# A one-core hybrid decoder step: early modulation slabs that hold two tiles of shift and scale, smaller tables at the start, and a turned score product in the GLA heads

## The chip, the cores and the metric

One core of one Trainium2 chip runs the whole step. The metric is the time of one execution in microseconds (us); a kernel is given by the median of its runs.

## The reference, cut to what matters

```python
mod = silu(c) @ w_ada + b_ada                      # c: 1 prompt row, 8 sample rows; w_ada 2048 x 12288
shift1, scale1, gate1, shift2, scale2, gate2 = split(mod, 6)
h = rmsnorm(x, norm1_g) * (1 + scale1) + shift1    # 256 prompt tokens, 32 sample tokens
qa, ka, va, qb, kb, vb, r, glr = split(h @ w_in)
oa = mix_a(...)                                    # dilated attention with a T5 relative bias, samples read a cache
ob = mix_b(...)                                    # 4 GLA heads: decay, causal product q k, states
x = x + gate1 * (concat(norm(oa), norm(ob) * silu(r)) @ w_out)
h2 = rmsnorm(x, norm2_g) * (1 + scale2) + shift2
x = x + gate2 * conv_ffn(h2)                       # w_up, causal conv, silu, w_down
```

Outputs are y for prompt and samples, the new keys and values, GLA states and conv rows. The depth is 1, and all is float32.

## The kernel before, in words

The program is written by hand for each engine: the order on an engine is the order of its code, and semaphores tie the engines. The 2048 features are 16 tiles of 128. Tokens (288 columns) are the moving operand of every large product; weights are split into a high part (`whi`, ScalarE) and a low part (`wlo`, VectorE), and `three` (lines 949 to 951) issues three matmuls per tile of weights. A chunk is 4 tiles by 256 columns of weights: 24 matmuls.

**The opening.** SyncE loads the constants `con` (identity, head halves, ones, then the masks `causal`, `causal_s`, `own_batch`, and `sum_groups`), x, and the first slabs of `w_ada`. TensorE turns x (`x_turns`, line 854), then works on slabs 0 to 7 of `w_ada` (`early_slab`), on the bias tables (`biases`, lines 862 to 866, from tables that GpSimd loads into `temp`), and between them on products of constants whose result nobody reads (`idle_products`, line 881). The small semaphore counts of a `Steps` object name each hand-over, and `upto` waits for one.

**Early slabs.** Shift and scale of the first norm come in 4 groups of 512 features each. Group i has 8 slabs of 1 MB: four of shift, four of scale, each with 4 of the 16 tiles by 512 columns. In a slab the four tiles go to four groups of 32 array columns (`ada_slab`, line 893), so that four partial sums lie on 4 x 32 PSUM rows. `ada_rows` (line 1507) copies 512 columns to `mrow`, and `ada_turn` (line 907) multiplies by `sum_groups`, which adds the four parts and turns them: 4 matmuls with 9 columns, once for shift (`turn_a`) and once for scale (`turn_b`). Then VectorE adds the bias (`mod`), scales the normalized tiles (`norm_group`) and splits them; with group 0 done the first chunk can start. Slabs 8 to 31 run between the first 20 chunks, where the table `ADA_AT` puts them. Slabs 12 to 31 are issued by ScalarE (`lead_load`, line 1524), each when an earlier slab is spent. The chunks' own loads come from SyncE (`in_load`, line 570). After chunk 20, late slabs (one tile by 2048 columns, `tile_slab`, line 900) carry the other four sixths of `w_ada`.

**ScalarE's loop** does per chunk j: copies of old results, `in_hi(j + 3)` (line 1488, waits for the slab of `w_in` and a free buffer), slab loads, row copies, then its part of a head or a pair.

**GLA heads.** Four heads run beside chunks 28 to 60; `head(h, r)` is step r of head h on each engine, a step per chunk. In steps 4 and 5 TensorE makes the causal products of 8 stretches of 32 queries: `att(h, c)` has the keys `ki[c]` as the weights and 32 query columns as the moving operand, in one matmul (line 1039) or, from c = 4, two (lines 1039 and 1042), so that they come out with keys on rows. VectorE multiplies them by `causal` (line 2163) in step 6. TensorE adds squares in step 8 (line 1119), after all eight new states are done; line 1061 starts the next head.

**GpSimd** loads the small tables first, waits for the third group's turn, and then loads `wglr`, `wg2` and the first states (lines 742 to 752).

## Time and profile before

| | |
|---|---|
| median of 3 runs | 1621.52 us (1619.14 to 1622.28) |
| the profiled execution's own time | 1621.12 us |
| its span | 1619.6 us |
| TensorE busy | 1582.2 us, 98% of the span |
| VectorE, ScalarE, GpSimd busy | 890.9, 664.2, 76.9 us |
| moved by DMA | 370.81 MB, mean 229 GB/s |
| share of the chain that ended last | PE 83%, DMA 5%, issue 5%, DVE 4%, ACT 2% |
| granted TensorE clock, mean | 0.994 |

Times in the profile count from the start of the span. A matmul of float32 has two records (two passes), so an "x8" is 4 matmuls of the program. A record ends when its pipeline has drained, so two that follow each other overlap; the cost of a group on a busy TensorE is from its start to the start of what follows.

### The profile page before, as it was taken

The page shows a single profiled execution, that of the slowest core. Times are in us where ns is not written, and L with a number is a line of the kernel's source. Part 1 is how long each engine was busy: PE and PEld are TensorE (multiplying, and loading weights), DVE is VectorE, ACT ScalarE, POOL GpSimd, SP SyncE. Part 2 cuts the span into 40 slices and gives each one's busy share as a digit, 9 for nine tenths or more (in the row PEclk, how much of TensorE's full clock was granted, in tenths as well). Part 3 has the DMA queues.
Part 4 walks back from the last instruction along what each step waited for, and adds up shares of the span by engine and source line. Part 5 has one row for each costly group of instructions (what it writes and reads, how often), then busy time and mean ns, then how long its engine had stood idle before and what let it go on. Part 6 is the DMA issues. An engine that isn't in the chain of part 4 may idle for free.

```text
span 1619.6 us, 29366 instructions
## 1 busy us (share of the span) xinstructions
PE 1582.2 (98%) x12352; PEld 1430.2 (88%) x12352; DVE 890.9 (55%) x1504; ACT 664.2 (41%) x925; POOL 76.9 (5%) x135
## 2 busy tenths in 40 slices
PE   8899999999999998999999999999999999999997
PEld 4677888888877765997999999999999999999997
DVE  3555555555665654657445455454555556656563
ACT  3332333343445434435334333343433445545452
POOL 2010000000111000000000000000000000000000
PEclk8999999999999999999999999999999999999999
DMA  9998877778877999866644444555545455555450
GB/s 339 375 384 298 307 258 260 270 278 282 288 255 278 335 397 368 310 231 235 229 163 158 158 161 156 182 163 175 161 158 168 148 170 179 160 177 179 158 183 27
DMA packets 240881, 370.81 MB, mean 229 GB/s; under 512 B 7809, under 2 KB 192483, under 8 KB 232553
## 3 DMA queue, kind: packets, MB, share of 16 engines
q1 hardware_dynamic: 216032, 279.88, 51.1%
q10 hardware_dynamic: 17538, 71.45, 11.8%
q0 software_dynamic: 7184, 17.64, 3.3%
q8 instruction: 98, 1.61, 0.4%
q14 instruction: 29, 0.24, 0.0%
HBM read 359.06 MB, written 9.88 MB: 228 GB/s over the span
## 4 chain that ended last, share of the span: by engine, by line
PE 83%; DMA 5%; issue 5%; DVE 4%; ACT 2%; SPq 1%; POOL 0%; ACTq 0%; POOLq 0%; DVEq 0%
PE ps L949 23%; PE ps L950 22%; PE ps L951 22%; PE ps L900 3%; PE ps L1197 2%; DMA ring<-in_w_in 1%; DMA ring<-in_w_ada 1%; DMA vals<-in_w_ada 1%; SPq L548 1%; DMA proj<-in_w_ada 1%; DVE wlo L2041 1%; PE ps L1212 1%; PE ps L1243 1%; PE ps L893 1%; DMA ring<-in_w_out 1%
## 5 line engine op out<-in xcount | busy, mean ns | idle before, releaser
L949 PE MATMUL ps<-hhi,whi 128*128 128x288 f32 x3120 | 929.7, 298 | 1.7 <-DVE hlo L2033 0.7
L950 PE MATMUL ps<-hlo,whi 128*128 128x288 f32 x3120 | 917.8, 294 | 0.0
L951 PE MATMUL ps<-hhi,wlo 128*128 128x288 f32 x3120 | 917.6, 294 | 0.0
L949 PEld LDWEIGHTS ps<-hhi,whi 128*128 128x128 f32 x3120 | 586.0, 188 | 40.1 <-issue 35.3
L950 PEld LDWEIGHTS ps<-hlo,whi 128*128 128x128 f32 x3120 | 586.2, 188 | 0.8
L951 PEld LDWEIGHTS ps<-hhi,wlo 128*128 128x128 f32 x3120 | 586.0, 188 | 0.0
L1897 DVE TENSOR_TENSOR wlo<-ring,whi 128x1024 fp32r<-128x1024 f32 x178 | 212.2, 1221 | 84.7 <-ACT whi L1479 84.3
L1479 ACT ACTIVATE whi<-ring 128x1024 fp32r<-128x1024 f32 x178 | 184.5, 1056 | 156.3 <-PE ps L951 156.3
L2041 DVE TENSOR_TENSOR wlo<-ring,whi 128x1024 fp32r<-128x1024 f32 x96 | 117.2, 1223 | 124.2 <-ACT whi L1488 124.0
L1488 ACT ACTIVATE whi<-ring 128x1024 fp32r<-128x1024 f32 x96 | 100.8, 1054 | 157.5 <-PE ps L951 125.4
L2541 DVE TENSOR_TENSOR wlo<-ring,whi 128x1024 fp32r<-128x1024 f32 (+1 forms) x94 | 105.7, 1131 | 56.0 <-ACT whi L1817 56.0
L1817 ACT ACTIVATE whi<-ring 128x1024 fp32r<-128x1024 f32 (+1 forms) x94 | 91.8, 980 | 73.8 <-PE ps L951 73.7
L2459 DVE TENSOR_TENSOR hlo<-proj,hhi 128x1152 fp32r<-128x1152 f32 (+3 forms) x56 | 60.9, 1100 | 47.5 <-ACT hhi L1766 46.6
L1766 ACT ACTIVATE hhi<-proj 128x1152 fp32r<-128x1152 f32 (+3 forms) x56 | 52.7, 954 | 49.7 <-PE ps L951 49.7
L2480 DVE TENSOR_SCALAR work<-work,small 128x304 f32<-128x304 f32 x44 | 17.3, 436 | 99.2 <-ACT work L1778 99.2
L2492 DVE TENSOR_TENSOR proj<-ps,work 128x512 f32<-128x512 f32 x22 | 15.2, 692 | 84.5 <-PE ps L951 84.5
L1777 ACT ACTIVATE work<-ps 128x512 f32<-128x512 f32 x22 | 13.2, 599 | 109.2 <-PE ps L951 109.2
L900 PE MATMUL ps<-ring,c 128*32 128x512 f32 x416 | 50.2, 599 | 0.0
L2298 DVE COPY kcT<-ps 128x512 f32<-128x512 f32 x40 | 27.3, 690 | 35.0 <-PE ps L1197 35.0
L1677 ACT ACTIVATE whi<-ring 128x1024 fp32r<-128x1024 f32 x30 | 30.9, 1052 | 35.4 <-DMA ring<-in_w_out 24.3
L2483 DVE SCALAR_TENSOR_TENSOR work<-work,small 128x304 f32<-128x304 f32 x88 | 43.2, 532 | 1.6
L1197 PEld LDWEIGHTS ps<-con,ring 128*128 128x128 f32 x320 | 34.8, 140 | 8.3 <-issue 4.8
(318 smaller groups left out, 1115.7 us busy)
## 6 DMA issues: line engine op xcount, KB each, us to landing
ring<-in_w_up SPq DMA_DIRECT2D x88, 1024.0 KB, 5.1
ring<-in_w_ada ACTq DMA_DIRECT2D x58, 1024.0 KB, 7.2
ring<-in_w_in SPq DMA_DIRECT2D x48, 1024.0 KB, 8.8
ring<-in_w_down SPq DMA_DIRECT2D x32, 1408.0 KB, 6.6
ring<-in_cache_k_win SPq DMA_DIRECT2D x16, 1024.0 KB, 9.3
ring<-in_w_out SPq DMA_DIRECT2D x16, 1024.0 KB, 7.0
proj<-in_w_ada SPq DMA_DIRECT2D x14, 1024.0 KB, 9.4
ring<-in_w_ada SPq DMA_DIRECT2D x10, 1024.0 KB, 13.6
```

Source lines behind the costliest of these rows:

```text
L900: last = mm(ps[32 * g:32 * g + 32, bank, :], c32[:, k, :], rows[:, 512 * g:512 * g + 512], start=(k == 0), stop=(k == KD - 1))
L949: mm(out, w_hi, x_hi, start=start, stop=False)
L950: mm(out, w_hi, x_lo, start=False, stop=False)
L951: return mm(out, w_lo, x_hi, start=False, stop=stop)
L1197: last = turn(ps[:, 2 * (n % 2) + e, P * q:P * q + P], key_slab(t)[:, i // 2, c:c + P], ident)
L1479: f(whi[:, j % BUFS, 0:n], ring[:, s % SLOTS, n * (j % 2):n * (j % 2) + n], ACT.Copy).then_inc(hi_done, 1)
L1488: f(whi[:, j % BUFS, :].rearrange("p (k c) -> p k c", k=4), in_chunk_of(rows, j), ACT.Copy).then_inc(hi_done, 1)
L1817: f(whi[:, jj % BUFS, 0:n], ring[:, s % SLOTS, CHUNK * kc:CHUNK * kc + n], ACT.Copy).then_inc(hi_done, 1)
L1897: v.tensor_tensor(wlo[:, j % BUFS, 0:n], ring[:, s % SLOTS, n * (j % 2):n * (j % 2) + n], whi[:, j % BUFS, 0:n].bitcast(F32), ALU.subtract ...
L2041: v.tensor_tensor(wlo[:, j % BUFS, :].rearrange("p (k c) -> p k c", k=4), in_chunk_of(rows, j), whi[:, j % BUFS, :].bitcast(F32).rearrange ...
L2459: last = v.tensor_tensor(hlo[:, at:at + m, :], actT[:, k0:k0 + m, :], hhi[:, at:at + m, :].bitcast(F32), ALU.subtract)
L2541: v.tensor_tensor(wlo[:, jj % BUFS, 0:n], ring[:, (2 * kg + h) % SLOTS, CHUNK * kc:CHUNK * kc + n], whi[:, jj % BUFS, 0:n].bitcast(F32), A ...
```

## The change

Seven edits:

1. Slab s of a group now holds tiles 2(s mod 8) and 2(s mod 8) + 1, each with 512 columns of shift and 512 of scale. It comes in two DMAs, one per tile, with a semaphore each. TensorE makes 8 matmuls with 256 columns instead of 4 with 512; each group of 32 array columns has a stretch of its own (shift left, shift right, scale left, scale right) and adds over all 16 tiles. So there is one copy of 256 columns and one turn of 2 matmuls with 36 columns per group, in place of two copies of 512 and two turns of 4 matmuls with 9.
2. SyncE loads only the first 384 columns of `con`; the 424 columns of masks are loaded by GpSimd, after the fourth group's turn, ahead of `wglr`. GpSimd's wait for the third group becomes one for the fourth.
3. 640 columns of `mult_s` on 128 rows become 4 rows (`mult_t`) and a 4-row table that spreads them (`pick_t`); two more matmuls add them in PSUM, and VectorE copies where it added.
4. ScalarE's loop issues slab loads before `in_hi(j + 3)`, and late rows before both.
5. `att` has the 32 queries as the weights and up to 256 key columns as the moving operand: one matmul for each stretch, on its own 32 PSUM rows. ScalarE copies the 384 columns, and TensorE turns them by three transposes (`att_turns`).
6. The squares of step 8 wait for six of the eight new states, and the next head's first product for all.
7. `gate_rank` and what hangs on it move by one chunk; the idle products before the up-projection are 2 instead of 6.

```diff
-        keep = CONST_LAYOUT["sum_groups"][0] + NC9
+        front, keep = CONST_LAYOUT["causal"][0], CONST_LAYOUT["own_batch"][0] + NB
+        w_shift = a["w_ada"][0].rearrange("(k p) (h c) -> p k h c", p=P, h=6)[:, :, 0:2, :]
+        def ada_source(s, e):
+            at = 512 * (s // 8)
+            return w_shift[:, 2 * (s % 8) + e, :, at:at + 512]
+                for e in range(2):
+                    sp.dma_start(rows[:, 2 * e:2 * e + 2, :], ada_source(s, e)).then_inc(landed_in[e], 16)
-            sp.dma_start(con[:, :], a["tables"][:, 0:keep]).then_inc(con_in, 16)
+            sp.dma_start(con[:, 0:front], a["tables"][:, 0:front]).then_inc(con_in, 16)
...
+            pool.dma_start(temp[0:TS, ct - c0:c1 - c0], a["tables"][0:TS, ct:c1]).then_inc(temp_in, 16)
-            pool.wait_ge(*AT.upto("turn_b", 2))
+            pool.wait_ge(*AT.upto("turn", 3))
             pool.wait_ge(fill_c, 1)
+            pool.dma_start(con[:, front:keep], a["tables"][:, front:keep]).then_inc(masks_in, 16)
...
-                mm(ps[:, 1, :], rel_rows, tview("hot_s", P)[:, 0:512], start=True, stop=True)
+                mm(ps[:, 1, :], rel_rows, tview("hot_s", P)[:, 0:512], start=True, stop=False)
+                mm(ps[:, 1, :], tview("pick_t", TS), tview("mult_t", TS)[:, 0:512], start=False, stop=True)
...
+            def early_slab(s):
+                for e in range(2):
+                    k = 2 * (s % 8) + e
+                    pe.wait_ge(landed_in[e], landed)
+                    for g in range(4):
+                        c = 256 * (g % 2)
+                        last = mm(ps[32 * g:32 * g + 32, rows_at, 0:256], c32[:, k, :], rows[:, 2 * e + g // 2, c:c + 256],
+                                  start=(k == 0), stop=(k == KD - 1))
+            def early_turn(i):
+                for n in range(2):
+                    last = mm(out[:, :, n, :], mrow[:, P * n:P * n + P], nines, start=True, stop=True)
...
-                q = qp[:, 32 * c:32 * c + 32]
-                n = min(P, 32 * (c + 1))
-                last = mm(ps[0:n, 7, 32 * c:32 * c + 32], ki[c % 4][:, 0:n], q, start=True, stop=True)
-                if c >= 4:
-                    n = 32 * (c - 3)
-                    last = mm(ps[0:n, 7, P + 32 * c:P + 32 * c + 32], ki[c % 4][:, P:P + n], q, start=True,
-                              stop=True)
+                at, n, rows = P * (c // 4), 32 * (c + 1), slice(32 * (c % 4), 32 * (c % 4) + 32)
+                mm(ps[rows, 7, at:at + n], qp[:, 32 * c:32 * c + 32], ki[c % 4][:, 0:n], start=True,
+                   stop=True).then_inc(*RT.step(f"att{c}"))
+            def att_turns(h):
+                pe.wait_ge(*RA.upto("att_rows", h))
+                for n in range(3):
+                    last = turn(ps[:, 7, P * n:P * n + P], att_rows[:, P * n:P * n + P], ident)
...
+                    pe.wait_ge(*RV.upto("state1", h - 1))
                     mm(ps[:, 7, 0:TOK], wg2[:, P * h:P * h + P], glrT, start=True, stop=True).then_inc(*RT.step("z"))
...
-                    pe.wait_ge(*RV.upto("state1", h))
+                    pe.wait_ge(*RV.upto("state_half", h))
...
-                    idle_products(2, 6)
+                    idle_products(2, 2)
```

TensorE, from slab 4 to the first chunk (line 862 and on are the bias products; `vals` holds slabs 4 to 7), before:

```order
L893 MATMUL ps<-vals,c 32x512 x4
L862 MATMUL ps<-proj 16x512
L865 MATMUL ps<-proj 128x512
L866 MATMUL ps<-proj 128x160
L907 MATMUL ps<-con,mrow 128x9 x4
L893 MATMUL ps<-vals,c 32x512 x8
L881 MATMUL ps<-con 128x256 x3
L893 MATMUL ps<-vals,c 32x512 x4
L881 MATMUL ps<-con 128x256
L907 MATMUL ps<-con,mrow 128x9 x4
L881 MATMUL ps<-con 128x256 x8
```

and changed:

```order
L927 MATMUL ps<-vals,c 32x256 x8
L878 MATMUL ps<-proj 16x512
L881 MATMUL ps<-proj 128x512
L882 MATMUL ps<-proj 128x512
L883 MATMUL ps<-proj 128x32
L884 MATMUL ps<-proj 128x128
L885 MATMUL ps<-proj 128x128
L927 MATMUL ps<-vals,c 32x256 x16
L900 MATMUL ps<-con 128x256 x3
L927 MATMUL ps<-vals,c 32x256 x8
L900 MATMUL ps<-con 128x256
L937 MATMUL ps<-con,mrow 128x4x9 x2
```

The turn behind the bias products is gone, one matmul with 512 columns and one with 128 are added there, and the last turn has 2 matmuls.

ScalarE, from its first chunk of the loop (line 1488 is `in_hi`, 1524 the slab load, 1536 a copy of a result), before:

```order
L1536 ACTIVATE proj<-ps 128x288
L1488 ACTIVATE whi<-ring 128x1024
L1524 DMA ring<-in_w_ada 128x4x512
L1536 ACTIVATE proj<-ps 128x288
L1488 ACTIVATE whi<-ring 128x1024
L1524 DMA ring<-in_w_ada 128x4x512
L1524 DMA proj<-in_w_ada 128x4x512
```

and changed:

```order
L1549 ACTIVATE proj<-ps 128x288
L1538 DMA ring<-in_w_ada 128x2x512 x2
L1505 ACTIVATE whi<-ring 128x1024
L1549 ACTIVATE proj<-ps 128x288
L1538 DMA ring<-in_w_ada 128x2x512 x2
L1538 DMA proj<-in_w_ada 128x2x512 x2
L1505 ACTIVATE whi<-ring 128x1024
```

Each slab load stands ahead of the `whi` of its chunk, and is two DMAs.

TensorE, step 5 of a head (line 1089 and on are the state and the samples' rows), before:

```order
L1039 MATMUL ps<-proj 128x32
L1042 MATMUL ps<-proj 96x32
L1039 MATMUL ps<-proj 128x32
L1042 MATMUL ps<-proj 128x32
L1089 MATMUL ps<-proj 128x256
L1090 MATMUL ps<-proj 128x256
L1094 MATMUL ps<-ring 32x256 x8
```

and changed:

```order
L1052 MATMUL ps<-proj 32x160
L1052 MATMUL ps<-proj 32x192
L1052 MATMUL ps<-proj 32x224
L1052 MATMUL ps<-proj 32x256
L1106 MATMUL ps<-proj 128x256
L1107 MATMUL ps<-proj 128x256
L1111 MATMUL ps<-ring 32x256 x8
L1059 MATMUL ps<-con,proj 128x128 x3
```

Eight small products became four wider ones, and three transposes stand at the end of the step.

## Rows read from the trace of the kernel before

**Rows 1.** The page: busy time, share of the span and instructions of each engine.

```profile
PE 1582.2 (98%) x12352; PEld 1430.2 (88%) x12352; DVE 890.9 (55%) x1504; ACT 664.2 (41%) x925; POOL 76.9 (5%) x135
```

**Rows 2.** Waits of TensorE, whole span: us in total, times, longest.

```profile
PE ps L893 <- DMA proj<-in_w_ada: 3.1, 3, 1.7
PE ps L893 <- DMA ring<-in_w_ada: 2.4, 2, 1.4
...
PE ps L1119 <- DVE ring L2107: 1.5, 2, 0.7
```

**Rows 3.** Stretches: us, PE, PEld, DVE, ACT, POOL busy, PEclk, DMA share, GB/s.

```profile
58.20:62.00 3.80, 3.80 (x30) 2.80 (x29) 2.71 (x4) 3.80 (x6) 0.00 (x0) 1.00 0.76 254
112.00:116.00 4.00, 4.00 (x36) 3.56 (x28) 1.69 (x4) 1.30 (x3) 0.00 (x0) 1.00 1.05 386
124.00:128.00 4.00, 4.00 (x31) 3.00 (x31) 1.69 (x4) 1.29 (x2) 0.00 (x0) 1.00 1.02 269
152.00:156.00 4.00, 4.00 (x33) 4.00 (x32) 3.23 (x10) 1.22 (x3) 0.00 (x0) 1.00 0.24 90
```

**Rows 4.** DMA issues up to 150 us: count, KB each, median us to landing.

```profile
proj<-in_tables POOLq DMA_DIRECT2D x1, 720.0 KB, 8.1
con<-in_tables SPq DMA_DIRECT2D x1, 408.5 KB, 3.7
```

**Rows 5.** Timeline of TensorE, slab 4 to the first chunk: start us, us.

```profile
31.63 1.06 PE L893 MATMUL ps<-vals,c 128*32 128x512 f32 x8 [2.25 <-DMA vals<-in_w_ada]
32.63 1.03 PE L862 MATMUL ps<-proj 32*16 32x512 f32 x2
...
34.82 0.95 PE L907 MATMUL ps<-con,mrow 128*128 128x9 f32 x8
...
37.63 1.56 PE L881 MATMUL ps<-con 128*128 128x256 f32 x6
39.31 1.06 PE L893 MATMUL ps<-vals,c 128*32 128x512 f32 x8
...
41.18 1.03 PE L907 MATMUL ps<-con,mrow 128*128 128x9 f32 x8 [0.18 <-ACT mrow L1507]
...
46.44 0.37 PE L949 MATMUL ps<-hhi,whi 128*128 128x288 f32 x1 [0.68 <-DVE hlo L2033]
```

**Rows 6.** Timeline of ScalarE, the high part of chunk 4.

```profile
58.20 1.06 ACT L1488 ACTIVATE whi<-ring 128x1024 fp32r<-128x1024 f32 x1 [7.91 <-DMA ring<-in_w_in]
```

**Rows 7.** Timeline of TensorE, a slab at 137 us.

```profile
137.11 1.07 PE L893 MATMUL ps<-ring,c 128*32 128x512 f32 x8 [1.38 <-DMA ring<-in_w_ada]
```

**Rows 8.** Timeline of TensorE, a late turn.

```profile
270.36 0.98 PE L977 MATMUL ps<-con,mrow 128*128 128x36 f32 x8
```

**Rows 9.** Timeline of TensorE in the sample attention.

```profile
543.10 1.07 PE L1212 MATMUL ps<-kcT,proj 128*32 128x256 f32 x16
543.98 0.48 PE L1225 MATMUL ps<-qkS,proj 128*32 128x32 f32 x32
544.39 1.97 PE L1197 MATMUL ps<-con,ring 128*128 128x128 f32 x16
546.29 1.07 PE L1212 MATMUL ps<-kcT,proj 128*32 128x256 f32 x16
```

**Rows 10.** Timeline of TensorE, steps 4 and 5 of the first head.

```profile
201.23 0.97 PE L1039 MATMUL ps<-proj 128*32 128x32 f32 x8
...
206.00 0.30 PE L1039 MATMUL ps<-proj 128*128 128x32 f32 x2
...
207.84 0.68 PE L1089 MATMUL ps<-proj 128*128 128x256 f32 x2
```

**Rows 11.** Timeline of VectorE, the keys of step 5.

```profile
205.08 1.23 DVE L2103 TENSOR_TENSOR proj<-proj 128x160 f32<-128x160 f32 x4
```

**Rows 12.** Timeline of TensorE, chunk 3 of the up-projection.

```profile
767.63 0.37 PE L949 MATMUL ps<-hhi,whi 128*128 128x288 f32 x1 [0.42 <-DVE wlo L1897]
```

**Rows 13.** A stretch at its start, columns as in rows 3.

```profile
750.00:755.00 5.00, 5.00 (x34) 4.74 (x33) 4.96 (x15) 3.02 (x7) 0.00 (x0) 1.00 1.01 421
```

More of the change, by code:

```diff
@@ L114, in constants @@
         new.append(np.where(b[:, None] == a[None] // TS, m, NEG))
-    add("mult_s", np.concatenate([old] + new, 1).astype(np.float32))
+    add("mult_s", np.concatenate(new, 1).astype(np.float32))
     return np.concatenate(parts, 1)
@@ L339, in build @@
         NL = [st("norm1_lower", "l0", "l1", "l2", "l3"), st("norm2_lower", "l0", "l1", "l2", "l3")]
-        AT = st("ada_tensor", "turn_a", "turn_b")
-        AA = st("ada_scalar", "rows_a", "rows_b")
+        AT = st("ada_tensor", "turn")
+        AA = st("ada_scalar", "rows")
         AV = st("ada_vector", "mod")
@@ L483, in out_slab, with ada_place @@
             return t % SLOTS, t // SLOTS * 16 + 16 - EVEN_LESS
+        half_in = [sem(f"slot_half_in{t}") for t in range(SLOTS)]
+        first_half = [sem(f"first_slab_half_in{t}") for t in range(4)]
+        lead_half = [sem(f"lead_slab_half_in{t}") for t in range(2)]
+        def ada_place(s):
+            place, slot, landed = ada_home(s)
+            rows = slab(slot, 4, 512) if place == 0 else (first_rows, lead_rows)[place - 1][slot]
+            return rows, ((full, first_in, lead_in)[place][slot], (half_in, first_half, lead_half)[place][slot]), landed
+        def ada_source(s, e):
+            at = 512 * (s // 8)
+            return w_shift[:, 2 * (s % 8) + e, :, at:at + 512]
         ADA_AT = [0, 1, 1, 2, 3, 3, 4, 5] + [6 + 7 * s // 8 for s in range(8)] + [13 + 7 * s // 8 for s in range(8)]
@@ L543, in ada_load @@
             def ada_load(s):
-                i, at = s // 8, 512 * (s // 8) + D * (s // 4 % 2)
-                place, slot, _ = ada_home(s)
-                dst = slab(slot, 4, 512) if place == 0 else (first_rows, lead_rows)[place - 1][slot]
-                sp.dma_start(dst, w_ada[:, 4 * (s % 4):4 * (s % 4) + 4, at:at + 512]
-                             ).then_inc((full, first_in, lead_in)[place][slot], 16)
+                rows, landed_in, _ = ada_place(s)
+                for e in range(2):
+                    sp.dma_start(rows[:, 2 * e:2 * e + 2, :], ada_source(s, e)).then_inc(landed_in[e], 16)
             def half_load(w, s, column, slot):
@@ L888, in norm2_sum @@
                 last.then_inc(*NT[1].step(f"s{n}"))
-            def ada_slab(bank, s, rows):
-                for k in range(4):
-                    last = mm(ps[32 * k:32 * k + 32, bank, :], c32[:, 4 * (s % 4) + k, :], rows[:, k, :],
-                              start=(s % 4 == 0), stop=(s % 4 == 3))
-                last.then_inc(raw_used, 1)
             def tile_slab(bank, k, rows):
@@ L902, in tile_slab @@
                 last.then_inc(raw_used, 1)
[L904 to L923 removed]
+            def early_slab(s):
+                i, rows_at = s // 8, 7 if s // 8 % 2 else 3
+                if i and s % 8 == 0:
+                    pe.wait_ge(*AA.upto("rows", i - 1))
+                rows, landed_in, landed = ada_place(s)
+                for e in range(2):
[5 more added lines that the diff above has]
+                                  start=(k == 0), stop=(k == KD - 1))
+                last.then_inc(raw_used, 1)
+            def early_turn(i):
+                pe.wait_ge(*AA.upto("rows", i))
+                pe.wait_ge(*AV.upto("mod", i - 1))
+                pe.sem_inc(row_turns, 1)
+                out = ps[:, 5, 0:8 * NC9].rearrange("p (g n c) -> p g n c", g=4, n=2)
+                for n in range(2):
+                    last = mm(out[:, :, n, :], mrow[:, P * n:P * n + P], nines, start=True, stop=True)
+                last.then_inc(*AT.step("turn"))
             idle_products(6, 6)
@@ L1518, in lead_load @@
             def lead_load(a):
-                place, slot, _ = ada_home(8 + a)
-                dst = slab(slot, 4, 512) if place == 0 else lead_rows[slot]
-                at = 512 * (1 + a // 8) + D * (a // 4 % 2)
+                rows, landed_in, _ = ada_place(8 + a)
                 act.wait_ge(raw_used, a + 5)
-                act.dma_start(dst, w_ada[:, 4 * (a % 4):4 * (a % 4) + 4, at:at + 512]
-                              ).then_inc(full[slot] if place == 0 else lead_in[slot], 16)
+                for e in range(2):
+                    act.dma_start(rows[:, 2 * e:2 * e + 2, :], ada_source(8 + a, e)).then_inc(landed_in[e], 16)
             def late_load(r):
@@ L2179, in head @@
                         last = new_state(b)
+                        if b == 5:
+                            last.then_inc(*RV.step("state_half"))
                     last.then_inc(*RV.step(f"state{r - 7}"))
```

110 lines of the change are left out of this document (48 added, 62 removed).

## The prediction

> **What bounds the kernel now.** I read the page first: TensorE is busy for 98% of the span [rows 1]. Time that leaves its stream after the opening is therefore gained, if nothing it waits for comes later, and a faster ScalarE or VectorE alone gains nothing. The list of its waits comes next: after the first product the longest are for slabs of `w_ada`, 3.1 + 2.4 = 5.5 us [rows 2], all before 140 us; the other that the change touches is 1.5 us for the GLA states. The stretches say why the slabs are late: the DMA engines are full (share 1.05 at 386 GB/s at 112 us), lose rate beside GpSimd's small packets (269 GB/s at 124 us), and have nothing to do from 152 us on (share 0.24) [rows 3]. So there are three regimes: an opening that ends with a latency chain, 95 us in which DMA and TensorE are nearly equal, and TensorE alone after that.
>
> **The start of the first chunk.** SyncE's constants shrink from 408.5 KB to 384 columns x 128 rows x 4 bytes = 192 KB, GpSimd's table from 720 KB to 400 KB plus 12 KB for the rows of 4 [rows 4]. That is 0.53 MB less ahead of slab 7, at 386 GB/s [rows 3] 1.4 us. Slab 4, which waited for its load until 31.63 [rows 5], starts 1.4 us earlier. From there to slab 7 TensorE has its own queue: it ended its idle products at 37.63 + 1.56 = 39.2 and slab 7 began at 39.31, so TensorE was only just ahead of the load. In that queue a turn goes (0.88 us, as long as the one between 34.82 and slab 5) and a matmul of 512 columns (0.96, from 32.63 to the next) and one of 128 (about 0.27) come. Slab 7 starts 1.4 + 0.88 - 0.96 - 0.27 = 1.1 us earlier, and its load no longer decides. Behind it the copy has 256 columns instead of 512 and the turn 2 matmuls instead of 4: the wide turn's 8 records last 0.98 against 0.95 for the narrow one's [rows 8, 5], so the price is by the matmul, and half a turn is 0.44 us. With 0.2 for the copy (an estimate) this gives 0.6. VectorE's work from the turn to the first product (46.44) [rows 5] stays. First chunk: **1.7 us** earlier, between 0.9 (if slab 7 keeps its slack) and 2.2.
>
> **From there to chunk 21.** TensorE's share: after the first group there were six turns of 0.88, now three of 0.44: 5.3 - 1.3 = 4.0 us. The slabs themselves I take at no change. The nearest row has exactly the new form, 128x32 weights and 256 columns in four groups of array columns: 16 records from 543.10 to 543.98, 0.88 us [rows 9], where a slab's 8 records of 512 columns take 1.00 (31.63 to 32.63). DMA's share: the 1.4 us of bytes, and a hole. From 58.2 to 62 us the engines moved 254 GB/s [rows 3], 1.3 us lost, because ScalarE stood 7.91 us before the `whi` of chunk 4, waiting for `w_in` [rows 6], with the slab loads behind it. Edit 4 puts them ahead. So up to about 90 us the loads gain 1.4 + 1.3 = 2.7, and TensorE, which could gain 1.7 + 1.3, is held to 2.7. After 90 us it waited once more, 1.38 us at 137 us [rows 7], when GpSimd's loads had thinned the stream. These move behind the fourth turn (about 143 us), next to the stretch in which DMA is nearly idle. There the 0.22 MB of masks and 1.2 MB of `wglr`, gates and states need some 6 us of DMA time, which 152 to 160 us have free; nothing of it is used before `gate_rank`, now at chunk 25, some 20 us later. So this wait goes, and four of the six old turns lie here, two of the new: 3.5 - 0.9 = 2.6. Sum up to chunk 21: 2.7 + 2.6 + 1.4 = **6.7 us**. Bounds: 1.4, only the bytes; and 1.7 + 4.0 + 5.5 = 11.2, every wait gone.
>
> **The heads.** Step 4's products took 0.8 us (0.97 with the drain), step 5's 1.84 (206.00 to 207.84) [rows 10]: 2.64 us. New: 320 moving columns in step 4, 832 in step 5. At 1024 columns in 0.88 us [rows 9], four groups at once, these are 0.27 and 0.72. Three transposes are 6 records; 16 such took 544.39 to 546.29 [rows 9], so 0.71. Together 1.70, a gain of 0.94 per head, **3.8 us** for four. The keys don't hold it: VectorE had made the last at 206.31 [rows 11]. ScalarE's new copy of 384 columns lies beside 2 us of other products, and VectorE's masking, which starts some 1 us later, ends long before step 6. Other bound: if the groups did not overlap, 1152 columns x 4 x 0.86 ns = 4.0 plus 0.7 is 2.0 more than before, a loss of 8 us.
>
> **The states.** The waits of line 1119 [rows 2] go: two new states fewer are awaited, some 0.8 us by VectorE, and the next head's first product stands behind the sum, which covers it. **1.5 us**, at worst 0.
>
> **Costed at nothing.** VectorE's copies replace additions of the same size. Four idle products fewer: TensorE then meets the normalized tiles as they come. VectorE is busy 4.96 of 5 us there [rows 13], and TensorE already had to wait for it at 767.63 [rows 12], so what starts earlier waits longer. If that cover is gone it is 1.7 us. ScalarE's doubled issues are covered by its 59% of idle time.
>
> **A rule against the change.** Every early slab becomes two DMAs of 512 KB. The rows here have 1 MB slabs at 386 GB/s [rows 3], in queues that are never empty, so that an end of one DMA lies beside another; I take the same rate for halves. The Trainium skill ("DMA: Bandwidth & Descriptors", Bandwidth) says to batch DMAs to 1 MiB or more to reach 75% of peak, and gives 138 GB/s for 64 KB; by that the slabs would come more slowly; the third rival below prices that with numbers of this kernel. No run here shows 512 KB halves with these 2 KB pieces.
>
> Sum: 6.7 + 3.8 + 1.5 = 12.0 us off the profiled execution's 1621.1, 1609.1; the median of the runs shown is 0.4 above that execution, so **1609.5 us**.
>
> **Rivals.**
> - *The loads keep the opening.* The two-queue order helps one side and hurts the other, or the masks and states now hit the loads of chunks 22 to 26; up to chunk 21 only 1.4 us come. For it: DMA is full until 150 us. Against: the hole at 58 us and the empty stretch at 152. 1609.5 + 5.3 = 1614.8. Chance 0.17.
> - *The head products don't overlap.* Their widths differ, and each waits for its own keys. For it: 8 us of loss as above, in place of 3.8. Against: the row of equal form [rows 9]. 1609.5 + 11.8 = 1621.3, no change. Chance 0.05.
> - *Halved DMAs cost* (the Trainium skill's rule above, as a mechanism of this kernel). 32 DMAs more before 137 us. The loads have 2.7 us and the 5 us of GpSimd's thinned stretch to spare, and 5.3 are gained later; the result turns to slower by 0.2% when each extra DMA costs over (7.7 + 5.3 + 3.2) / 32 = 0.5 us. At 0.7 us they cost 22: 1621.5 + 22 - 13 = 1631. Against: the full queues. Chance 0.03.
> - *The change acts as stated*, within 4 us of the sum. Chance 0.75.
>
> **How the numbers follow.** A measurement tells 0.2%, 3.2 us, from no change. Faster by that: 0.75 + 0.17 = 0.92, less 0.01 for a half-clock stretch; same 0.06; slower 0.03. The low end is the bound of 11.2 in place of 6.7, 1605; the high end takes in the first rival with a quarter off its heads and states, 1617. Beyond are the other two, and a rest.
>
> **What would show it.** First chunk at 44.7 us; a turn of 4 records for each group, about 0.44 us; slabs of 16 records in 0.9 to 1.0 us; DMA over 370 GB/s from 56 to 62 us; no wait near 137 us; chunk 21 some 6.7 us earlier. Steps 4 and 5 of a head 1.7 us with the transposes; no wait of the sum for states. Slabs of over 1.2 us, or a DMA rate under 350 GB/s from 60 to 110 us, would make it wrong.

## The result and the profile after

The changed kernel is **0.2% slower**: 1624.44 us median (1620.14 to 1628.16, 20 runs) against 1620.73 for the kernel before (1618.34 to 1623.72, 20 runs), ratio 1.0021 with a 95% interval of 1.0015 to 1.0028. The forecast was 1609.5, range 1605 to 1617. Its profiled execution took 1623.34 us, span 1621.8.

The page of the changed kernel, busy times:

```profile
PE 1578.5 (97%) x12538; PEld 1429.9 (88%) x12538; DVE 890.0 (55%) x1504; ACT 662.5 (41%) x925; POOL 78.1 (5%) x137
```

TensorE has 3.7 us less to do than in [rows 1], and the span is 2.2 us longer (1619.6 before), so it stands idle for 5.9 us more. The waits of TensorE in the changed kernel say for what (total, times, longest, in us):

```profile
PE ps L963 <- DVE hlo L2047: 4.3, 2, 3.6
PE ps L900 <- DMA con<-in_tables: 4.0, 1, 4.0
PE ps L963 <- ACT proj L1549: 2.7, 1, 2.7
PE ps L1178 <- DVE proj L2226: 2.7, 2, 1.8
PE ps L1169 <- DVE proj L2267: 2.2, 2, 1.1
...
PE ps L1145 <- DVE proj L2223: 1.9, 2, 0.9
...
PE ps L927 <- DMA ring<-in_w_ada: 1.2, 2, 0.7
```

The waits for the slabs of [rows 2] fell from 5.5 us to 1.2, and the wait of the sum for the GLA states is gone. In their place TensorE waits for *computed* data: a copy by ScalarE, `hlo` of the second feature group, and intermediate results of the pairs.

To see where the difference arises I take the start of the first product of a chunk. Every kernel has the same 24 products per chunk in the same order, so chunk n of one stands against chunk n of another. In us from the span's start:

| chunk | before | changed | changed - before |
|---|---|---|---|
| 0 | 46.44 | 44.55 | -1.89 |
| 3 | 60.33 | 61.27 | +0.94 |
| 6 | 79.08 | 75.17 | -3.90 |
| 8 | 89.89 | 91.31 | +1.42 |
| 21 | 150.88 | 149.83 | -1.05 |
| 61 | 359.70 | 355.68 | -4.03 |
| 64 | 372.45 | 368.42 | -4.03 |
| 98 | 639.98 | 642.33 | +2.35 |
| 384 | 1583.17 | 1585.48 | +2.31 |

Two places give away what the rest gains: the two stalls up to chunk 8, and the stretch with the pairs, chunks 64 to 98, which takes 6.4 us longer, 5.2 of them by chunk 93.

**The stall before chunk 8.** ScalarE, VectorE and TensorE in the changed kernel (timeline: start, us, engine, line, operation; in brackets the idle time before it and what ended it):

```profile
80.97 4.96 ACTq L1538 DMA_DIRECT2D ring<-in_w_ada  x4
86.03 1.06 ACT L1505 ACTIVATE whi<-ring 128x1024 fp32r<-128x1024 f32 x1 [6.58 <-issue]
```

```profile
87.12 1.23 DVE L2055 TENSOR_TENSOR wlo<-ring,whi 128x1024 fp32r<-128x1024 f32 x1 [6.61 <-ACT whi L1505]
88.27 0.29 DVE L1939 TENSOR_TENSOR modT<-ps,small 128x36 f32<-128x36 f32 x2
...
90.72 1.56 DVE L2047 TENSOR_TENSOR hlo<-proj,hhi 128x288 fp32r<-128x288 f32 x4
```

```profile
91.31 0.58 PE L963 MATMUL ps<-hhi,whi 128*128 128x288 f32 x1 [3.56 <-DVE hlo L2047]
```

ACTq is ScalarE's queue at its DMA issues. Four half slabs took 4.96 us to issue, ahead of `whi` for chunk 10. VectorE makes `wlo` for chunk 10 before it scales feature group 1, so it stood 6.61 us, and TensorE, which at chunk 8 needs group 1 and not chunk 10's weights, waited 3.56 us. It then got the lower of its two clocks, 1.2 GHz, for a time: two successive stretches of the changed kernel, the columns as in [rows 3] (the granted clock, 0.86 and 0.71, is the third number from the end):

```profile
88.00:92.00 4.00, 0.69 (x3) 0.72 (x4) 3.83 (x14) 1.81 (x6) 0.00 (x0) 0.86 1.05 386
92.00:96.00 4.00, 4.00 (x23) 3.85 (x22) 1.86 (x3) 0.98 (x1) 0.00 (x0) 0.71 1.05 386
```

Chunk 8 took 91.31 to 97.01, 5.70 us against 4.35 before: 1.3 us more. In the kernel before, the same loads stood behind `whi` and were two issues in 1.23 us.

**The stall before chunk 3.** The splitting of chunk 4, which stood at 58.20 in [rows 6], comes at 59.77, and the copy that frees chunk 3's PSUM bank is behind it:

```profile
59.77 1.06 ACT L1505 ACTIVATE whi<-ring 128x1024 fp32r<-128x1024 f32 x1 [11.37 <-DMA ring<-in_w_in]
...
60.73 0.39 ACT L1549 ACTIVATE proj<-ps 128x288 f32<-128x288 f32 x1
```

In the four kernels with the early loads ahead (changed, and 3, 4 and 8 below) this splitting starts at 59.8 to 60.9 us, in those with the loads behind, where it waits for `w_in` too, at 57.0 to 58.2. That slabs issued from 49 us on take DMA time from this `w_in` fits, but no run separates it. The hole at 58.2 to 62 us did get smaller (309 GB/s against 254), but most of that is not of edit 4: with it undone (kernel 1 below) the engines moved 293 GB/s there.

**The pairs.** What ScalarE waited for between 375 and 500 us, first in the kernel before, then in the changed one:

```profile
ACT whi L1488 <- PE ps L951: 24.4, 10, 5.0
```

```profile
ACT whi L1505 <- PE ps L912: 16.6, 5, 5.4
ACT whi L1505 <- PE ps L965: 12.0, 6, 3.6
...
ACT mrow L1514 <- PE ps L912: 1.5, 1, 1.5
```

Line 912 is the product of a late slab. Before, the splitting waited only for its own buffer (line 951, or 965 after the change). Now a late load stands ahead of it, and waits for a slab's products, which TensorE does behind the 24 products of a chunk. ScalarE's part of the pair, and VectorE's behind it, come later with the splitting, and TensorE's waits for them (lines 1178, 1169 and 1145 in the list above) grow.

### The profile page after: what moved, and what is told of

Its sections match the earlier page's. It is cut to its first block, busy times and chain, and to the rows that moved or that the text cites. A ratio compares the mean times of both kernels' runs of the same rounds, so it can differ in the third digit from the quotient of the medians.

```text
span 1621.8 us, 29765 instructions
## 1 busy us (share of the span) xinstructions
PE 1578.5 (97%) x12538; PEld 1429.9 (88%) x12538; DVE 890.0 (55%) x1504; ACT 662.5 (41%) x925; POOL 78.1 (5%) x137
## 4 chain that ended last, share of the span: by engine, by line
PE 81%; DMA 6%; issue 5%; DVE 4%; ACT 2%; SPq 1%; ACTq 0%; POOL 0%; DVEq 0%; POOLq 0%
PE ps L963 23%; PE ps L964 22%; PE ps L965 22%; PE ps L912 3%; DMA proj<-in_cache_v_win 2%; DMA ring<-in_w_in 1%; PE ps L1214 1%; PE ps L927 1%; DVE wlo L2055 1%; DMA ring<-in_w_ada 1%; ACT whi L1505 1%; DMA vals<-in_w_ada 1%; SPq L563 1%; PE ps L1229 1%; PE ps L1260 1%
## 5 line engine op out<-in xcount | busy, mean ns | idle before, releaser
L2476 DVE TENSOR_TENSOR hlo<-proj,hhi 128x1152 fp32r<-128x1152 f32 (+3 forms) x56 | 60.9, 1100 | 47.5 <-ACT hhi L1780 46.5
```

The costliest lines, as they stand in the source:

```text
L2476: last = v.tensor_tensor(hlo[:, at:at + m, :], actT[:, k0:k0 + m, :], hhi[:, at:at + m, :].bitcast(F32), ALU.subtract)
```

## The experiments

My theory from these rows, A: **edit 4, the new order in ScalarE's loop, makes the splitting of `w_in` late and costs 10 to 12 us, and the rest of the change gains about what was forecast.** Rivals: the doubled number of DMA issues (edit 1) costs it wherever they stand; or the new work of heads and pairs (edits 5 and 6) shifted the later stretch. Each kernel was timed beside runs of the kernel before, not all in one session; here is what came of them, in us (medians; chunk starts are of the one profiled execution of each):

| kernel | median | ratio to before, 95% | chunk 8 | 21 | 61 | 64 | 98 |
|---|---|---|---|---|---|---|---|
| before | 1620.2 to 1621.7 | 1 | 89.89 | 150.88 | 359.70 | 372.45 | 639.98 |
| changed | 1624.44 | 1.0021 (1.0015-1.0028) | 91.31 | 149.83 | 355.68 | 368.42 | 642.33 |
| 1 order undone | 1611.86 | 0.9940 (0.9926-0.9955) | 89.37 | 146.54 | 351.21 | 363.96 | 630.80 |
| 2 early loads back | 1621.12 | 0.9998 (0.9989-1.0007) | 89.56 | 146.75 | 352.42 | 365.17 | 640.52 |
| 3 late loads, rows back | 1616.21 | 0.9966 (0.9955-0.9977) | 92.72 | 149.87 | 354.59 | 367.33 | 634.58 |
| 4 order alone | 1630.44 | 1.0055 (1.0041-1.0068) | 90.64 | 150.15 | 361.60 | 374.34 | 647.54 |
| 5 heads alone | 1617.65 | 0.9981 (0.9972-0.9991) | 89.61 | 150.91 | 355.52 | 368.27 | 632.46 |
| 6 halves alone | 1623.56 | 1.0020 (1.0011-1.0029) | 89.91 | 153.18 | 361.86 | 374.61 | 642.89 |
| 7 rows ahead | 1614.12 | 0.9962 (0.9949-0.9975) | 88.13 | 145.31 | 350.05 | 362.80 | 630.04 |
| 8 one burst back | 1610.84 | 0.9937 (0.9924-0.9950) | 89.60 | 146.78 | 351.52 | 364.27 | 632.17 |
| 9 late loads one later | 1616.91 | 0.9984 (0.9973-0.9996) | 90.25 | 147.43 | 359.43 | 372.18 | 640.38 |
| 10 GpSimd at the third | 1618.07 | 0.9983 (0.9974-0.9992) | 89.50 | 151.53 | 356.11 | 368.86 | 635.47 |
| 11 six idle products | 1612.07 | 0.9948 (0.9934-0.9961) | 89.86 | 147.04 | 352.05 | 364.80 | 634.55 |

**How far one trace can be read.** The profiled execution lies up to 4.5 us from the median of its kernel (kernel 9: 1621.42 against 1616.91; kernel 5: 1613.92 against 1617.65). Where that comes from can be seen. Up to chunk 8 the kernels 1, 2, 7, 9 and 11 run the same program, and start it at 88.13 to 90.25 us. Chunks 93 to 98 hold the attention of the samples, and take 114.4 to 120.0 us whatever the edit. Between these two places most chunks of the same program repeat to 0.01 us, except for chunk 41 (8.1 to 8.5 us in the kernels 1, 3, 7, 8, 10 and 11): chunks 8 to 21 take 57.15 to 57.18 in seven of the variants. So a difference in the opening or behind chunk 93 needs more than 2 us to count, and one in the middle does not. The pairs are best read from chunk 64 to 93: 149.7 to 150.7 us in the ten kernels in which no late load waits ahead of the splitting, against 154.97 (changed), 156.57 (kernel 4) and 158.40 (kernel 2).

**1. The order undone.** In the changed kernel, ScalarE's loop:

```diff
-                if j - 1 in LATE_AT[KD - 1::KD]:
-                    late_rows(LATE_AT.index(j - 1) // KD)
+                if j + 3 < CH_OUT:
+                    in_hi(j + 3)
...
-                if j + 3 < CH_OUT:
-                    in_hi(j + 3)
...
+                if j - 1 in LATE_AT[KD - 1::KD]:
+                    late_rows(LATE_AT.index(j - 1) // KD)
                 for h in range(H_B):
```

> The changed kernel with edit 4 alone undone: ScalarE's loop splits w_in (in_hi) first, issues the slab loads behind it, and copies late rows at its end, as the kernel before does. Theory A (the new order makes the splitting of w_in late, by loads in front of it in ScalarE's queue, and costs 10 to 12 us that hide the gain of the rest): about 1613 us, ratio to before 0.995; the wait of PE before chunk 8 for hlo (3.6 us) and the one for the projection copy before chunk 3 (2.7 us) gone, and chunks 64 to 98 take as long as before (they lose 6.4 us to it in the changed kernel). Rival B (twice as many DMA issues on ScalarE and in the rings cost it, wherever they stand): 1619 to 1624, ratio 0.999 to 1.002. Rival C (the loss in chunks 64 to 98 is of the heads' and pairs' new work, edits 5 and 6): chunks 64 to 98 still lose 6 us, about 1618.

Measured: 1611.86 us, 9.8 below the kernel before of the same runs and 12.6 below the changed one. Chunks 64 to 98 take 266.84 us, against 267.53 before and 273.91 in the changed kernel. The waits of TensorE up to 150 us, with the order undone:

```profile
PE ps L900 <- DMA con<-in_tables: 4.1, 1, 4.1
PE ps L870 <- DMA proj<-in_x_sample: 2.1, 1, 2.1
PE ps L927 <- DMA ring<-in_w_ada: 0.9, 1, 0.9
PE ps L927 <- DMA proj<-in_w_ada: 0.9, 2, 0.7
PE ps L963 <- DVE hlo L2047: 0.7, 1, 0.7
```

The 3.6 and the 2.7 us are gone, and `hlo` is back to the 0.7 that it had before. Theory A as stated holds; both rivals had named other numbers. (In this execution TensorE waited 2.1 us for the sample tokens, and chunk 0 began at 48.95. By chunk 8 it was at 89.37, as early as kernel 2, whose chunk 0 began at 45.04: what the start gains or loses hardly reaches chunk 8.)

**2 and 3. The two halves of edit 4.** Kernel 2 is the changed one with `lead_load`'s loop moved behind `in_hi`. Kernel 3 keeps it ahead, and puts `late_load` and `late_rows` where they were:

```diff
-                for a_ in range(4, 24):
-                    if ADA_AT[a_ - 4] == j - 1:
-                        lead_load(a_)
...
                 if j + 3 < CH_OUT:
                     in_hi(j + 3)
+                for a_ in range(4, 24):
+                    if ADA_AT[a_ - 4] == j - 1:
+                        lead_load(a_)
```

> The changed kernel with only the early slabs' loads put back behind the splitting of w_in; late loads and late rows stay ahead of it. Theory A: the opening's stalls at chunks 3 and 8 go (chunk 21 starts 5 to 6 us earlier than in the changed kernel), the loss from chunk 64 to 98 stays: about 1618 to 1619, ratio 0.998 to 0.999. Rival B: chunk 21 no earlier than 149.8, about 1624.

> The changed kernel with the late loads put back behind the splitting of w_in and the late rows at the loop's end; the early slabs' loads stay ahead. Theory A: chunk 21 starts as in the changed kernel (149.8), but chunks 64 to 98 take no longer than before: about 1618, ratio 0.998. Rival C: 1624, the chunks from 64 on lose 6 us as in the changed kernel.

Measured: 1621.12 and 1616.21, where I had 1618 to 1619 and 1618. The places are as expected, the sizes not: kernel 2 brings chunk 21 forward by 3.1 us, where I had said 5 to 6, and keeps the loss of the pairs (275.35 us for chunks 64 to 98); kernel 3 starts chunk 21 at 149.87 and does the pairs in 267.25. So the early loads ahead cost some 4 us, the late loads and rows some 9 (1616.21 and 1621.12 less 1611.86), 13.6 by themselves and 12.6 together.

**4. The order alone**, the same edit in the kernel before.

> The kernel before with edit 4 alone: slab loads and late rows ahead of the splitting of w_in in ScalarE's loop, nothing else changed. Theory A: 1626 to 1632, ratio 1.004 to 1.007, with waits of PE for hlo or the projection copy in the opening and a loss of some 6 us in chunks 64 to 98. Rival B (the halved loads' issues cost it, not their place): within 2 us of before, ratio 0.999 to 1.001. My forecast's own reading of edit 4 (a hole at 58 to 62 us closed, 1.3 us): 1620, ratio 0.999.

Measured: 1630.44, 8.7 us *slower* than before, in the range of theory A. Chunks 64 to 98 take 273.20 us, 5.7 more, and chunks 21 to 61 2.6 more. But chunk 21, at 150.15, starts 0.7 us *earlier* than before: the same early loads ahead of the splitting made chunk 3 start 2.0 us later and chunk 8 0.75, and by chunk 21 nothing of it was left. The burst at the same place, ScalarE in kernel 4:

```profile
82.31 2.95 ACTq L1524 DMA_DIRECT2D ring<-in_w_ada  x2
85.36 1.06 ACT L1488 ACTIVATE whi<-ring 128x1024 fp32r<-128x1024 f32 x1 [4.45 <-PE ps L893]
```

Two issues took 2.95 us, the four of the changed kernel 4.96, and TensorE waited 1.0 us at most for `hlo`, not 3.6. `whi` itself came only 0.7 us later in the changed kernel (86.03 against 85.36), and so did chunk 8; TensorE had got there earlier (chunk 6 at 75.17 against 77.03), so it stood longer, and chunk 8 at the lower clock took 5.70 us against 4.32. So the order alone explains the loss in the pairs. The one in the opening needs more of the change beside it: the halved DMAs, which lengthen the burst, and whatever brings TensorE there earlier. A kernel with the order and the halves only was not run.

**6. The halves alone.** In the kernel before, each early slab in two DMAs:

```diff
-                act.dma_start(dst, w_ada[:, 4 * (a % 4):4 * (a % 4) + 4, at:at + 512]
-                              ).then_inc(full[slot] if place == 0 else lead_in[slot], 16)
+                act.dma_start(dst[:, 0:2, :], w_ada[:, k:k + 2, at:at + 512]
+                              ).then_inc(full[slot] if place == 0 else lead_in[slot], 16)
+                act.dma_start(dst[:, 2:4, :], w_ada[:, k + 2:k + 4, at:at + 512]
+                              ).then_inc(half_in[slot] if place == 0 else lead_half[slot], 16)
```

(and the same on SyncE, and a second wait ahead of the products).

> The kernel before with every early slab loaded by two transfers of half the bytes (two tiles each, same rows and columns) on a semaphore each, and nothing else changed. Forecast and theory A: the bytes decide, not the number of transfers, and ScalarE's extra issues stand behind the splitting of w_in: 1620.5 to 1622.5, ratio 1.000. Rival B (the doubled issues cost it wherever they stand; forecast's rival priced it at some 10 us): 1625 or more, ratio 1.002 up.

Measured: 1623.56, 3.4 us slower than the 1620.17 of the kernel before in the same session. My range was missed; of the rival's two bounds the ratio of 1.002 was reached and the 1625 us not, so doubled issues do cost something by themselves. The halves alone do nothing to chunk 8 (89.91), and cost 2.6 us at one point, ahead of chunk 17. ScalarE and TensorE there:

```profile
127.71 3.99 ACTq L1535 DMA_DIRECT2D proj<-in_w_ada  x1
131.80 0.60 ACT L1515 ACTIVATE mrow<-ps 128x512 f32<-128x512 f32 x1 [4.40 <-issue]
```

```profile
132.54 1.03 PE L914 MATMUL ps<-con,mrow 128*128 128x9 f32 x8 [1.95 <-ACT mrow L1515]
...
134.91 0.61 PE L957 MATMUL ps<-hhi,whi 128*128 128x288 f32 x1
135.31 0.44 PE L958 MATMUL ps<-hlo,whi 128*128 128x288 f32 x1
135.55 0.44 PE L959 MATMUL ps<-hhi,wlo 128*128 128x288 f32 x1
```

One issue stood 3.99 us in the queue, with the row copy of a turn behind it, and after the wait the records follow each other at 0.24 us, where the full clock shows 0.13. In the kernel before, the one issue at that place took 0.37 us. So a doubled number of issues has a price where something urgent stands behind them on ScalarE. This place follows GpSimd's loads (117 to 122 us), as does the longest burst of kernel 10 below (two issues in 5.63 us at 125.74); with those loads moved to 147 us, kernel 1's two issues at 125.60 took 0.90. So part of the 3.4 us may be owed to GpSimd's loads, which the change moves away. The rate did not suffer: between 105 and 120 us the engines moved 381 GB/s in kernel 6 against 383 before, and 387 with the order undone, in a stream of halves of 512 KB and `w_in` slabs of 1 MB. By the Trainium skill's advice of DMAs of 1 MiB or more ("DMA: Bandwidth & Descriptors", Bandwidth) the slabs would have come more slowly; the measured rate does not bear that out here, and what the halves cost was time in the issuing queue.

**8. One burst back.** Kernel 3, but in the loop's step j = 7 (the four issues of 4.97 us) the early loads stand behind `in_hi`:

```diff
-                    if ADA_AT[a_ - 4] == j - 1:
+                    if ADA_AT[a_ - 4] == j - 1 and j != 7:
                         lead_load(a_)
                 if j + 3 < CH_OUT:
                     in_hi(j + 3)
+                for a_ in range(4, 24):
+                    if ADA_AT[a_ - 4] == j - 1 and j == 7:
+                        lead_load(a_)
```

> The changed kernel with late loads and late rows back behind the splitting of w_in, early loads ahead of it in every step of ScalarE's loop but the seventh, whose four issues of half a slab took 4.97 us ahead of the splitting for chunk 10. Theory A in its narrow form (that one burst makes the lower part of the second normalization group late by 3.6 us): chunk 8 starts some 3 us earlier than with all early loads ahead, total about 1613, against 1616.2 with the burst ahead and 1611.9 with all behind. If instead the loads ahead in the steps before it matter (they take DMA time from w_in), it stays at 1615 to 1616.

Measured: 1610.84; chunk 8 at 89.60, 3.1 us earlier than in kernel 3 (92.72). The stall before chunk 3 is still there (2.8 us), and the time is that of kernel 1 (ratio 0.9937 against 0.9940), where I had said about 1613. So, as far as the medians tell, this one burst was the whole of what the early loads cost. ScalarE in kernel 8:

```profile
82.38 1.06 ACT L1505 ACTIVATE whi<-ring 128x1024 fp32r<-128x1024 f32 x1 [1.00 <-DMA ring<-in_w_in]
82.89 4.97 ACTq L1538 DMA_DIRECT2D ring<-in_w_ada  x4
87.91 1.45 ACT L1480 ACTIVATE hhi<-proj 128x288 fp32r<-128x288 f32 x4 [4.47 <-DVE proj L2043]
```

The issues take as long as before, but `whi`, and with it VectorE's chain to `hlo`, is ahead of them.

**9. Late loads one chunk later.** Kernel 2 with

```diff
-                    if (LATE_AT[r - 2] if r >= 2 else ADA_AT[20 + r]) == j - 1:
+                    if (LATE_AT[r - 2] + 1 if r >= 2 else ADA_AT[20 + r]) == j - 1:
                         late_load(r)
```

> As the variant with early loads put back (late loads and late rows still ahead of the splitting of w_in), but each late load is issued one chunk later, when the slab whose buffer it takes has long been multiplied. Theory A, narrow form (the load waits on ScalarE for products that TensorE issues behind a head's or pair's work, and the splitting for three chunks on waits behind it): the 7.8 us lost between chunks 64 and 98 go, total 1611 to 1613, ratio 0.994 to 0.995. Rival (the loads' issue time or their traffic ahead of w_in costs it): as before this edit, 1619 to 1622. Rival C (chunks 64 to 98 slow down through the copy of late rows): also 1619 to 1622.

Measured: 1616.91, between the two. The stretch of the pairs, 64 to 93, takes 150.66 us, against 158.40 in kernel 2 and 150.12 in kernel 1: the loss there is gone, with the late loads still ahead of the splitting. It was the wait of the load that cost it, as the theory's narrow form says, and not the copy of late rows, which is ahead in both. But chunks 21 to 61 take 212.01 us where kernel 1 needs 204.68, which no theory had foreseen. This may overstate it: the profiled execution took 1621.42 us, and seven of the kernel's ten took 1616.07 to 1617.09, so part of the 7.3 us may belong to the slower executions only. The largest part, 3.3 us, falls in chunk 41. ScalarE, kernel 9 and then kernel 1:

```profile
244.17 1.06 ACT L1505 ACTIVATE whi<-ring 128x1024 fp32r<-128x1024 f32 x1 [5.46 <-DMA ring<-in_w_in]
245.13 1.53 ACT L1574 ACTIVATE proj<-proj 128x160 f32<-128x160 f32 x4
```

```profile
240.90 1.06 ACT L1505 ACTIVATE whi<-ring 128x1024 fp32r<-128x1024 f32 x1 [3.70 <-DMA ring<-in_w_in]
...
241.87 1.53 ACT L1574 ACTIVATE proj<-proj 128x160 f32<-128x160 f32 x4
```

The keys of a head's step 5 (line 1574) stand behind a splitting that waits for `w_in`, which lands later in kernel 9; TensorE waited 2.7 us for these keys, against 0.9 in kernel 1. Why `w_in` lands later there I have not separated (other loads at other times, or a `wlo` that frees its slot later).

**7. Rows ahead.** Kernel 1 with the copy of late rows ahead of `in_hi`:

```diff
+                if j - 1 in LATE_AT[KD - 1::KD]:
+                    late_rows(LATE_AT.index(j - 1) // KD)
                 if j + 3 < CH_OUT:
                     in_hi(j + 3)
...
-                if j - 1 in LATE_AT[KD - 1::KD]:
-                    late_rows(LATE_AT.index(j - 1) // KD)
```

> The changed kernel with the order undone, except that the copy of late rows stands ahead of the splitting of w_in, as the change has it; all loads stay behind. If the loads ahead of the splitting cost the time: as with the order wholly undone, 1611 to 1613. If the wait of the copy of rows for its 16 products holds up the splitting: 1614 to 1619. If the earlier rows help (PE's wait of 1.4 us for them at 270 us goes): 1610.5.

Measured: 1614.12, at the lowest edge of the second expectation, while its profiled execution (span 1609.5) is 0.7 us shorter than kernel 1's (1610.2). From chunk 21 to the end of the pairs the two traces agree: 204.74 and 204.68 us for chunks 21 to 61, 150.22 and 150.12 for 64 to 93. So the trace shows no cost of the rows over 0.2 us. The medians are 2.3 us apart, and 3.8 if each is taken against the runs of the kernel before beside it; the intervals of the two ratios just overlap, so by the medians alone the question stays open.

**5. The heads alone**, edits 5 and 6 in the kernel before.

> The kernel before with edits 5 and 6 alone (the turned product of queries and keys, the copy of its rows and three transposes; the sum of squares waits for six of eight states, z for all). My forecast's terms: 3.8 us less for the four heads and 1.5 us less for the wait of the sum, so 1616.4, ratio 0.997. If the gain is only what was seen from chunk 32 to 61 with the order undone, 3.8: 1617.9, ratio 0.998. The rival of the forecast (the transposes and copy cost more than the products save): over 1622.

Measured: 1617.65, ratio 0.9981, 2.5 us less than the kernel before in its session; the rival's 1622 is excluded. In the trace, whose execution took 3.7 us less than the median, chunks 21 to 61 take 204.60 us against 208.82, 4.2 less. Step 5 of the first and of the third head, TensorE in kernel 1 (in kernel 5 the same groups take the same times to 0.01 us):

```profile
200.93 1.40 PE L1052 MATMUL ps<-proj 128*32 128x160 f32 x8
202.26 0.70 PE L1106 MATMUL ps<-proj 128*128 128x256 f32 x2
...
204.32 0.55 PE L1059 MATMUL ps<-con,proj 128*128 128x128 f32 x3
204.62 0.38 PE L963 MATMUL ps<-hhi,whi 128*128 128x288 f32 x1
```

```profile
290.12 0.61 PE L1052 MATMUL ps<-proj 128*32 128x160 f32 x8
290.66 0.70 PE L1106 MATMUL ps<-proj 128*128 128x256 f32 x2
```

and VectorE, which makes the keys, for the same two groups:

```profile
200.42 1.23 DVE L2117 TENSOR_TENSOR proj<-proj 128x160 f32<-128x160 f32 x4
```

```profile
286.76 1.23 DVE L2117 TENSOR_TENSOR proj<-proj 128x160 f32<-128x160 f32 x4
```

Where all keys are ready, step 5's products take 0.55 us from start to start, where they took 1.84 in the first head before [rows 10]: products of different widths on four groups of array columns overlap. But in the first head VectorE finishes the last key at 201.65, after TensorE has begun, and the products take 1.33 us, as they come. Chunk by chunk (kernel 5 against before): step 4 gains 0.5, 0.5, 0.0 and 0.5 us in the four heads, step 5 with its transposes 0.1, -0.3, 1.2 and 0.1, and the chunks with the sum of squares of the first and the last head 0.8 each.

**10. GpSimd at the third turn.** Kernel 1 with

```diff
-            pool.wait_ge(*AT.upto("turn", 3))
+            pool.wait_ge(*AT.upto("turn", 2))
```

> The changed kernel with the order undone, and GpSimd's loads of masks, w_glr, gates and states started after the third turn instead of the fourth. My forecast's term: the wait that stood at 137 us comes back, 1.4 us, so 1613.3 against 1611.9 with the order undone alone. If the stream of early slabs now has slack there: no difference, under 0.5 us at chunk 21.

Measured: 1618.07, 6.2 us more than kernel 1; chunk 21 at 151.53, 5.0 later. TensorE's waits for slabs between 44 and 200 us in kernel 10:

```profile
PE ps L927 <- DMA ring<-in_w_ada: 5.1, 3, 3.1
PE ps L927 <- DMA proj<-in_w_ada: 3.2, 3, 1.6
```

The longest, 3.1 us, lies ahead of chunk 17, one chunk earlier than the 1.38 us in [rows 7], and a stretch of lower clock follows. From chunk 8 to 21 this kernel takes 62.04 us, kernel 1 57.17, the kernel before 60.99, and kernel 6 (halves, the old turns, GpSimd's loads at the third group) 63.28. The whole 4.9 us against kernel 1 lie in chunks 16 and 17.

**11. Six idle products.** Kernel 1 with `idle_products(2, 6)` in place of `idle_products(2, 2)`.

> The changed kernel with the order undone, and 6 idle products ahead of the MLP's first units as before instead of 2. My forecast costed the four fewer at nothing, VectorE's normalization being the bound behind them: chunk 131 starts as with 2, total 1611 to 1613. If they held TensorE up: 1.3 us more (0.33 us each), 1613.2, and the trace shows chunk 131 that much later; if fewer of them cost a half clock instead: this one is faster.

Measured: 1612.07, no difference. Chunks 127 to 131 take 25.94 us with six, 25.93 with two and 25.94 before.

## Why the prediction was wrong

**Edit 4, the step that failed.** I read it as a gain alone: "Edit 4 puts them ahead", 1.3 us from the hole at 58 us. I asked what the loads stood behind, and never what would stand behind the loads. Kernel 1 prices the edit at 12.6 us in the changed kernel and kernel 4 at 8.7 in the kernel before. The rows to see it in were there. ScalarE stood in front of `whi` for 7.91 us [rows 6], so its queue was one with waits in it, and `whi` is what VectorE's whole chain stands behind. And a load that waits for `raw_used` waits for a product that TensorE does behind a whole chunk's: a question for the code.

**"ScalarE's doubled issues are covered by its 59% of idle time."** False, and the second half of the same mistake. Idle time of the engine says nothing of its queue at a moment: four issues took 4.96 us and stood ahead of `whi` (the opening of the changed kernel), one took 3.99 ahead of a row copy (kernel 6, 3.4 us). Free time on average covers no work that stands in order ahead of urgent work.

**The rivals.** The third, that halved DMAs cost, came nearest, but by another mechanism than the one priced: not rate, as the Trainium skill's rule had it, but the issuing queue, and 3.4 us, not 22. The first rival began with "The two-queue order helps one side and hurts the other", but priced it as 5.3 us less of gain, in the loads up to chunk 21. None of them had edit 4 as the cause of a loss, or of anything at the late slabs.

**The start of the first chunk.** Forecast 1.7 us earlier. Measured 1.89 in the changed kernel and 1.1 to 1.9 in all variants of it but kernel 1 (which waited for the sample tokens): right, and by the way forecast, with slab 7 at 38.05 us in the changed kernel, 1.3 earlier than before (I had 1.1), and a last turn of 0.44.

**From there to chunk 21, the loads' 2.7 us.** Too much. With the early loads behind the splitting chunk 8 starts 0.4 us later to 1.8 earlier (kernels 1, 2, 7, 9, 10 and 11, in single executions), 0.45 earlier in the mean. So the earlier start was mostly lost again. The hole was not a cost of TensorE that an earlier load could give back: from 56 to 62 us the engines moved 296 GB/s before, 337 in the changed kernel (over 370 was my sign that this step is right) and 323 with the order undone, and in the changed kernel TensorE waited 2.7 us there.

**The turns' 2.6 us and the wait's 1.4.** Right, and each by itself. In kernel 1 the chunks 9, 13, 16 and 20, which held the old turns, are 0.8, 0.4, 0.8 and 0.4 us shorter than before, 2.4 together, and chunk 17, which held the wait at 137 us, 1.4. A turn takes 0.46 us (in the changed kernel, with what follows it):

```profile
117.72 0.53 PE L937 MATMUL ps<-con,mrow 128*128 128x36 f32 x4
118.18 1.07 PE L927 MATMUL ps<-ring,c 128*32 128x256 f32 x16
```

and a slab's 16 records 1.00 us (one slab after 38.05 us), the same as a slab before. Kernel 10 shows that the two terms hang together with the place of GpSimd's loads: it keeps the gain of chunks 9, 13 and 20 and loses it all in chunks 16 and 17, and is 1.0 us *slower* than before in this stretch. Whether that is because a faster TensorE waits longer for the same slabs, or because halves, masks and GpSimd's other loads meet there, no run separates. Against kernel 6, which has the halves and the old turns, it is 1.2 us faster.

**The heads, 3.8.** Mis-sized. By the chunks above, the products and transposes gained 2.6 us in kernel 5 and, by the same chunks, 2.2 in kernel 1 (the two differ in chunk 41 alone), not 3.8. Two things were wrong and in part made up for each other. The products themselves are cheaper than I had it: with all keys ready 0.35 us for step 4 and 0.55 for step 5, and 0.30 for three transposes, which leave three records where I had counted six; 1.20 in place of my 1.70. But "the keys don't hold it" was false. The row [rows 11] has the last key at 206.31, and step 5 began at 206.00 [rows 10]; products that took 1.84 us covered that, products of 0.55 don't. In three of the four heads they take 1.32 to 1.46 us, and in one of these TensorE waits another 0.9 us for the first key in kernel 1 (0.5 in kernel 5).

**The states, 1.5.** Right: the chunks with the sum are 0.78 and 0.79 us shorter, 1.6 together, in kernel 1 and in kernel 5, and the waits of 0.7 us are gone from the list.

**Idle products and copies, nothing.** Right: kernel 11, and the 25.93 us above.

Sum by this, for the trace of kernel 1: 0.5 up to chunk 8, 3.8 to chunk 21, 0.3 to chunk 32, 3.8 for heads and states, 0.7 from chunk 64 to 98 (where the spread of single executions is larger than that) = 9.1 us. In the medians kernel 1 gained 9.8, against my 12.0. The 2.2 to 2.9 that lack are the loads (2.2 short) and the heads' products (1.6 short), less what came unforeseen. The rest of the miss, 12.6 us, is edit 4.

Kernels 1 and 8, at 1611.86 and 1610.84 us (ratios 0.9940 and 0.9937), beat both the kernel before and the changed one. They differ from the latter by a few moved lines.

## What to carry to other kernels

When an instruction moves forward on an in-order engine, cost what it moves *past*: how long it may wait, and who waits for what stands behind it. Here one load waited for products that stood behind a whole chunk's, and the weights of three chunks later, and all that VectorE did after them, waited with it. A DMA issue on a compute engine's queue is such an instruction, and took up to 4 us here; cost it at the moment at which it stands, not by the engine's idle share. When a group of products gets shorter, ask again whether what it waits for is still ready: keys that 1.84 us of products had covered held up products of 0.55. And compare single traces chunk by chunk: most chunks repeat to 0.01 us, and the few that don't show where one execution can't be trusted.

## What the runs showed that I had not expected

- An issue of a DMA by ScalarE took from 0.37 us to 3.99 in the same kernel (line 1533 and line 1535 of kernel 6, at 122.95 and 127.71 us), with the DMA engines' share at 1.06 and 1.04; four took 4.96 us in the changed kernel at 80.97 us and 1.95 us at 119.31. So the share does not tell how long an issue will take.
- A stream with halves of 512 KB in it moved 381 to 387 GB/s, as much as one of 1 MB slabs (383 in the kernel before, 105 to 120 us).
- Three transposes of float32, 128 by 128, took 0.30 us from start to start, with three records.
- A stall of 3.56 us of TensorE was followed by a stretch at the lower of its two clocks (records at 0.24 us in place of 0.13), which made the next chunk 1.3 us longer.
